# Rounded matmuls that run through their columns backwards, in a two-layer pooling and mLSTM trunk

## The reference

```python
for i in range(DEPTH):                      # DEPTH = 2
    hn = rmsnorm(x, mix_pre_g[i])
    y = pool_mixer(hn, ...) if i % 2 == 0 else mlstm_mixer(hn, ...)
    x = x + rmsnorm(y, mix_post_g[i])
    hn = rmsnorm(x, ffn_pre_g[i])
    a = relu(hn @ w1[i])                    # 1024 x 4096
    x = x + rmsnorm((a * a) @ w2[i], ffn_post_g[i])
```

## Time and profile before

| | |
|---|---|
| median of 2 runs | 1902.47 us (1899.02 to 1905.91) |
| profiled execution, time | 1899.89 us |
| its span, first to last instruction | 1898.1 us |
| instructions in the profile | 24458 |
| TensorE matmuls, records | 8526 |
| granted TensorE clock, mean | 1.00 |

### The profile page before, as it was taken

How to read it: one execution, slowest core, us unless ns; L and a number is a source line. 1 busy time by engine, 2 the same in 40 slices (tenths; PEclk the granted TensorE clock), 3 DMA queues, 4 the chain that set the end, 5 groups by cost and what they waited for, 6 DMA issues and landing times.

```text
span 1898.1 us, 24458 instructions
## 1 busy us (share of the span) xinstructions
PE 1867.6 (98%) x8526; PEld 1533.9 (81%) x8526; DVE 1342.8 (71%) x2120; ACT 1068.3 (56%) x1825; POOL 89.8 (5%) x121
## 2 busy tenths in 40 slices
PE   9999999999999999999999999999999999999999
PEld 6678888888888888888878888777888888888886
DVE  5877565655778987786866868777665656577885
ACT  7655555563445546766766757645655555445533
POOL 0110000000000200010000100021000000000010
PEclk9999999999999999999999999999999999999999
DMA  5344343448633533353323442245243436853353
GB/s 211 114 159 171 122 169 136 168 181 323 220 96 97 195 115 111 100 175 98 104 80 100 131 157 90 78 150 193 90 167 139 166 140 239 304 179 99 111 194 128
DMA packets 79706, 284.80 MB, mean 150 GB/s; under 512 B 9408, under 2 KB 9664, under 8 KB 71136
## 3 DMA queue, kind: packets, MB, share of 16 engines
q1 hardware_dynamic: 64288, 239.96, 36.1%
q0 software_dynamic: 8320, 27.27, 4.3%
q10 hardware_dynamic: 6976, 16.01, 2.7%
HBM read 211.31 MB, written 71.89 MB: 149 GB/s over the span
## 4 chain that ended last, share of the span: by engine, by line
PE 87%; DVE 8%; ACT 2%; issue 2%; DMA 0%; SPq 0%; DVEq 0%; ACTq 0%
PE core L1024 5%; PE core L1025 5%; PE core L1026 5%; PE bank L807 5%; PE bank L809 5%; PE bank L808 5%; PE core L974 5%; PE core L976 5%; PE core L975 5%; PE bank L1025 4%; PE bank L1024 4%; PE bank L1026 4%; PE bank L976 4%; PE bank L975 4%; PE bank L974 4%; PE bank L907 2%
## 5 line engine op out<-in xcount | busy, mean ns | idle before, releaser
L1471 ACT CAST h_hi<-h_raw 128x512 fp32r<-128x512 f32 x188 | 116.7, 621 | 230.9 <-PE core L1026 140.0
L1835 DVE TENSOR_TENSOR w_lo<-raw,w_hi 128x1024 fp32r<-128x1024 f32 x132 | 161.1, 1222 | 118.0 <-ACT w_hi L1285 115.9
L807 PE MATMUL bank<-x_hi,w_hi 128*128 128x512 f32 x560 | 224.4, 401 | 3.6 <-issue 2.9
L1285 ACT CAST w_hi<-raw 128x1024 fp32r<-128x1024 f32 x132 | 137.9, 1045 | 145.6 <-PE bank L809 45.4
L809 PE MATMUL bank<-x_hi,w_lo 128*128 128x512 f32 x560 | 218.5, 390 | 0.0
L808 PE MATMUL bank<-x_lo,w_hi 128*128 128x512 f32 x560 | 218.2, 390 | 0.0
L2092 DVE TENSOR_TENSOR h_lo<-h_raw,h_hi 128x512 fp32r<-128x512 f32 x188 | 129.5, 689 | 109.6 <-ACT h_hi L1471 109.6
L1024 PE MATMUL core<-h_hi,w_hi 128*128 128x512 f32 x464 | 180.9, 390 | 1.7 <-DVE y L2158 1.6
L1026 PE MATMUL core<-h_hi,w_lo 128*128 128x512 f32 x464 | 180.5, 389 | 0.0
L1025 PE MATMUL core<-h_lo,w_hi 128*128 128x512 f32 x464 | 180.5, 389 | 0.0
L1986 DVE TENSOR_TENSOR w_lo<-sums,w_hi 128x512 fp32r<-128x512 f32 x104 | 71.7, 689 | 96.4 <-ACT w_hi L1313 93.6
(11 more groups left out here) (334 smaller groups left out, 4375.5 us busy)
## 6 DMA issues: line engine op xcount, KB each, us to landing
raw<-weights SPq DMA_DIRECT2D x132, 512.0 KB, 3.3
h_pair_dram<-y SPq DMA_DIRECT2D x26, 1792.0 KB, 6.6
h_raw<-h_pair_dram SPq DMA_DIRECT2D x182, 256.0 KB, 2.8
w<-second_pairs SPq DMA_DIRECT2D x24, 768.0 KB, 4.5
raw_odd<-first_pairs SPq DMA_DIRECT2D x14, 1024.0 KB, 7.1
x_scratch<-y POOLq DMA_DIRECT2D x48, 256.0 KB, 2.5
raw<-first_pairs SPq DMA_DIRECT2D x12, 1024.0 KB, 7.1
xold<-x_scratch POOLq DMA_DIRECT2D x40, 256.0 KB, 3.3
```

The source lines that it names most:

```text
L807: nc.tensor.matmul(o, a, hi(t), start=(k == 0), stop=False)
L1285: nc.scalar.copy(w_hi[:, ROW[u] * T:(ROW[u] + 2) * T], raw[:, (n % RAW) * BLK:(n % RAW + 1) * BLK]).then_inc(hi_ready, 1)
L1835: dve.tensor_tensor(w_lo[:, s], raw[:, (n % RAW) * BLK:(n % RAW + 1) * BLK], w_hi[:, s].bitcast(F32), ALU.subtract).then_inc(lo_ready, 1)
```

## The change

Every rounded matmul gets its moving operand and its output with the columns in reverse order. The stationary operand stays as it is, and so do the unrounded matmuls.

```diff
+        def back(tile):
+
+            return tile[:, ::-1]
+
...
-                    nc.tensor.matmul(o, a, hi(t), start=(k == 0), stop=False)
-                    nc.tensor.matmul(o, a, lo(t), start=False, stop=False)
-                    last = nc.tensor.matmul(o, b, hi(t), start=False, stop=(k == n - 1))
+                    nc.tensor.matmul(back(o), a, back(hi(t)), start=(k == 0), stop=False)
+                    nc.tensor.matmul(back(o), a, back(lo(t)), start=False, stop=False)
+                    last = nc.tensor.matmul(back(o), b, back(hi(t)), start=False, stop=(k == n - 1))
```

More of the change, by code:

```diff
@@ L870, in second_product @@
                             a, b = w_hi[:, c:c + P], w_lo[:, c:c + P]
-                            nc.tensor.matmul(o, a, hid_hi[:, k, :], start=(k == 0), stop=False)
-                            nc.tensor.matmul(o, a, hid_lo[:, k, :], start=False, stop=False)
-                            last = nc.tensor.matmul(o, b, hid_hi[:, k, :], start=False, stop=(k == FT - 1))
+                            nc.tensor.matmul(back(o), a, back(hid_hi[:, k, :]), start=(k == 0), stop=False)
+                            nc.tensor.matmul(back(o), a, back(hid_lo[:, k, :]), start=False, stop=False)
+                            last = nc.tensor.matmul(back(o), b, back(hid_hi[:, k, :]), start=False, stop=(k == FT - 1))
                         if k == FT - 1:
@@ L906, in plain_first @@
                         a, b = w_hi[:, r + k * P:r + (k + 1) * P], w_lo[:, r + k * P:r + (k + 1) * P]
-                        nc.tensor.matmul(o, a, XH(half, k), start=(k == 0), stop=False)
-                        nc.tensor.matmul(o, a, XL(half, k), start=False, stop=False)
-                        last = nc.tensor.matmul(o, b, XH(half, k), start=False, stop=(k == KT - 1))
+                        nc.tensor.matmul(back(o), a, back(XH(half, k)), start=(k == 0), stop=False)
+                        nc.tensor.matmul(back(o), a, back(XL(half, k)), start=False, stop=False)
+                        last = nc.tensor.matmul(back(o), b, back(XH(half, k)), start=False, stop=(k == KT - 1))
                         if k == KT - 1:
@@ L929, in plain_second @@
                         o = eight[d][:, :]
-                        nc.tensor.matmul(o, a, hp_hi[:, k, :], start=(k == 0), stop=False, skip_group_check=True)
-                        nc.tensor.matmul(o, a, hp_lo[:, k, :], start=False, stop=False, skip_group_check=True)
-                        ins = nc.tensor.matmul(o, b, hp_hi[:, k, :], start=False, stop=(k == PLAIN - 1), skip_group_check=True)
+                        nc.tensor.matmul(back(o), a, back(hp_hi[:, k, :]), start=(k == 0), stop=False, skip_group_check=True)
+                        nc.tensor.matmul(back(o), a, back(hp_lo[:, k, :]), start=False, stop=False, skip_group_check=True)
+                        ins = nc.tensor.matmul(back(o), b, back(hp_hi[:, k, :]), start=False, stop=(k == PLAIN - 1), skip_group_check=True)
                         if d == ds[-1]:
@@ L973, in pairs_first @@
                             a, b = w_hi[:, c:c + P], w_lo[:, c:c + P]
-                            nc.tensor.matmul(o, a, xh[:, k, :], start=(fresh and k == 0), stop=False, skip_group_check=True)
-                            nc.tensor.matmul(o, a, xl[:, k, :], start=False, stop=False, skip_group_check=True)
-                            last = nc.tensor.matmul(o, b, xh[:, k, :], start=False, stop=(final and k == 3), skip_group_check=True)
+                            nc.tensor.matmul(back(o), a, back(xh[:, k, :]), start=(fresh and k == 0), stop=False, skip_group_check=True)
+                            nc.tensor.matmul(back(o), a, back(xl[:, k, :]), start=False, stop=False, skip_group_check=True)
+                            last = nc.tensor.matmul(back(o), b, back(xh[:, k, :]), start=False, stop=(final and k == 3), skip_group_check=True)
                         last.then_inc(group_done, 1)
@@ L1023, in second @@
                         a, b = w_hi[:, c:c + P], w_lo[:, c:c + P]
-                        nc.tensor.matmul(o[:, :], a, hh, start=(fresh and first), stop=False, skip_group_check=True)
-                        nc.tensor.matmul(o[:, :], a, hl, start=False, stop=False, skip_group_check=True)
-                        ins = nc.tensor.matmul(o[:, :], b, hh, start=False, stop=(final and last), skip_group_check=True)
+                        nc.tensor.matmul(back(o[:, :]), a, back(hh), start=(fresh and first), stop=False, skip_group_check=True)
+                        nc.tensor.matmul(back(o[:, :]), a, back(hl), start=False, stop=False, skip_group_check=True)
+                        ins = nc.tensor.matmul(back(o[:, :]), b, back(hh), start=False, stop=(final and last), skip_group_check=True)
                         if d == ds[-1]:
```

## The result

The changed kernel takes 1941.2 us (median of 2 runs, 1940.2 to 1942.2) against 1902.5 us before: ratio 1.0206, 95% interval 1.0183 to 1.0228. Timed once more beside the kernel before, in more runs, it was 1.0202 (1.0185 to 1.0219), 1940.0 against 1900.5 us. So reading backwards costs 39 us, 2.0%. The time lies inside the range that was given, but the forecast was no change, and that is wrong.

What follows compares the result with a forecast made beforehand. The prediction took TensorE's count of rounded matmuls and their start distance to bound the kernel. 0 us for each of 7584 matmuls left the median, 1902 us, with a range of 1800 to 2010 us.

Steps and rivals of the forecast that it cites:

- TensorE's start distance sets the time: Whole kernel: TensorE busy 98% of the span, so the end follows rounded matmul starts, 0.2267 us apart.
- The count, 7584: Rounded matmuls in the kernel: 2528 instructions for the first of three passes, 7584 in all, unchanged by the edit.
- the parts at 0 us: Splits, evacuations, loads, stores, group-end signals and accumulating rewrites of a column: claimed to cost what they did, 0 us.
- I take 0 ns: Distance between rounded matmul starts with both patterns descending: claimed unchanged, 0 us for each of 7584; no change, chance 0.64.
- The fourteen groups: Profile groups of rounded matmuls; nine mean durations of 389 or 390 ns were taken to show tile and bank don't matter.
- The 13.4 ns over the columns: Each rounded matmul's start distance beyond 213.3 ns for 512 columns; losing it all would gain at most 101.6 us.
- The forecast is wrong if the chip takes columns in ascending pairs or blocks: Sign against the no-change forecast, on TensorE's column accesses; named as the one thing on which it rests; no size.
- The mild rival: A descending pattern costs 3 to 13 ns at each rounded matmul's start: 1925 to 2003 us, chance 0.07.
- The faster rival: The 13.4 ns come from moving and stationary tile addresses and go away when one is reversed: about 1808 us, chance 0.10.
- Half rate: Descending columns of moving tile or bank go at half rate, 202 ns more each: about 3418 us, chance 0.19.
- Unrounded matmuls stay 0.429 us apart in every case: Sign: the eight unrounded matmuls at the end keep 0.429 us; if they move too, the cause is not direction.
- The sum: 0 us for each of 7584 matmuls against the profiled execution's 1899.9 us; the median, 1902 us, was predicted.

## Why the prediction was wrong

- *TensorE's start distance sets the time.* Right. Each ns of it was worth 6 to 8 us here (39 us for 6.7 ns, 17 for 2.2, 274 for 40).
- *The count, 7584, and the parts at 0 us.* Right: the count of records, the clock and the busy time of VectorE and ScalarE did not move, and the bank's direction costs nothing (0.9994).
- *"I take 0 ns" for the distance.* This step failed. It rested on "a time that doesn't depend on which tile or bank is read looks set by the columns and something fixed for the instruction". The fourteen groups could not bear that out: in the kernel before, all moving tiles and all stationary blocks lie at multiples of 512 bytes, so every group had the same place of one against the other. The rows varied the tile and never the thing that mattered. What the runs showed in its place is 6.7 ns (233.3 against 226.7), set by where and in which order the moving tile is read against the stationary one. The 13.4 ns over the columns are the least of a scale that goes on to 20 ns in an ordinary place and 53 ns for words turned in sixteens.
- *"The forecast is wrong if the chip takes columns in ascending pairs or blocks; that is the one thing on which it rests and that no row of before shows"* was half of it. Pairs did not break the forecast: words turned within 16 bytes are free (226.7 ns). The order of the 16-byte lines did. But it rested on the place of the two tiles as well, which this sentence leaves out: a forward kernel with the weights 8 words off is as slow.
- *The mild rival, a fixed few ns (25 to 101 us, chance 0.07).* Its size was right: 6.7 ns. Its mechanism was not. A descending pattern has no price at its start, since the two-byte type, unrounded float32, lines turned in themselves and blocks of 128 pay none.
- *The faster rival* had named the right pair, the moving read and the load of the stationary tile ("forwards both") falling out of step, and had the sign wrong: the aligned forward pair is the cheap one. The argument that I brought against it ("an effect of addresses ought to vary with them", the slots) would have needed slots that differ. The price that the Trainium skill has for the two-byte type, 215.7 ns (TensorE: Matmul & The Clock Gate, "Wait — 56ns, not 53.3ns?"), agrees with the 215.8 ns here; the rounded form never came nearer to it than 226.7 ns.
- *Half rate (0.19)* did not come. The rule of the Trainium skill on PSUM's eight-byte lines (Advanced Engine Details and Errata, PSUM Cachelines), read by lines, agrees: with the bank alone backwards the distance stayed 227 ns.
- *"Unrounded matmuls stay 0.429 us apart in every case"* was right, and so was that idle time falls when each matmul is slower.
- *The sum.* With the distance right it would have been 51 us. The two profiled executions differ by 42 us (the medians by 39): idle time took 4.5, uneven rounded matmuls about 2, and as much went where a rounded matmul stands in front of a wait or an unrounded one.

That the partner of the moving read is the load of the stationary tile follows from the relative shifts. No run took that load away, so it isn't shown directly. Why the backward distance is the same for 72 and for 128 stationary columns, while the forward one rises from 226.7 to 230.4 ns, stays open. So do what makes sixteens so dear and why 4 words off cost 7 ns with changing weights and 1 ns with one tile.

## What to carry to other kernels

When a distance looks constant over many groups, ask what all of them share before calling it fixed: here it was an alignment, and one spacer of eight words in the wrong place costs 2%. With rounded matmuls at the end of the chain, measure the distance between starts in short stretches for a few offsets of moving against stationary tile, with the stationary block changing as it does in the kernel, and keep the best one through every later change of the allocation. Such a stretch by itself, read at the right offset, foretold each of the kernels, up to the part that idle time hides.

## What the hardware showed that I had not expected

- A rounded 128 x 512 matmul starts 226.7 to 229 ns behind the last one when both tiles begin at multiples of 64 words (256 bytes), and 229 to 237 ns behind it at most other offsets. The two-byte type needs 215.8 ns, and unrounded float32 429.2 ns for each record, both ways.
- The direction of the bank, the order of words in 16 bytes, and the order of 512-byte blocks of the moving tile are free. The order of the 16-byte lines in between costs 6.7 ns when they all run backwards, and 40 ns when they are turned in groups of four.
- One stretch turned the moving tile at every second matmul only. It took 6.90 us for 30, 230.0 ns, half the extra.

```profile
257.38 6.90 PE bank L173 x30
264.28 6.80 PE bank L176 x30
```

The second row is the bank turned at every second matmul: nothing.
